# A two-block network on one core: the recurrent stage in 64-column matrices, one 64x64 fp32 tile a head

## What is computed

```python
def step(S, inp):
    r_t, w_t, k_t, v_t, a_t, b_t = inp
    sa = jnp.einsum('bhij,bhj->bhi', S, a_t)
    S = S * w_t[:, :, None, :] + sa[..., None] * b_t[:, :, None, :] + v_t[..., None] * k_t[:, :, None, :]
    return S, jnp.einsum('bhij,bhj->bhi', S, r_t)
...
mean = jnp.mean(y, axis=-1, keepdims=True)
var = jnp.mean(jnp.square(y - mean), axis=-1, keepdims=True)
y = ((y - mean) * lax.rsqrt(var + GN_EPS)).reshape(B, L, D_INNER)
y = y * ln_w.astype(jnp.float32) + ln_b.astype(jnp.float32)
```

## Time and profile before

| | |
|---|---|
| median of the three runs | 2902.48 us |
| profiled execution: its own time | 2891.52 us |
| its span, first to last instruction | 2889.5 us |
| granted clock of TensorE, mean | 0.931 |
| TensorE matmul busy | 2475.3 us (86%) |
| VectorE busy | 1648.8 us (57%) |
| GpSimd busy | 1468.6 us (51%) |
| ScalarE busy | 965.5 us (33%) |

### The profile page before, as it was taken

One profiled execution on the slowest core, in us unless ns is written; L12 is line 12 of the kernel. 1 busy time (PEld: TensorE's weight loads), 2 busy tenths in 40 slices (PEclk: granted clock), 3 DMA queues, 4 the chain that ended last, 5 costly groups with the idle time before them and its releaser, 6 DMA issues.

```text
span 2889.5 us, 45055 instructions
## 1 busy us (share of the span) xinstructions
PE 2475.3 (86%) x15926; PEld 2161.8 (75%) x15926; DVE 1648.8 (57%) x2307; ACT 965.5 (33%) x2235; POOL 1468.6 (51%) x907
## 2 busy tenths in 40 slices
PE   6799999897888887888877869999998689978876
PEld 5689898797787777878877859677778577666555
DVE  6766666667666676666765264144442417337755
ACT  1532323354455454445442122223331111111331
POOL 1466666644443354444338748312218579775334
PEclk8899999898999998889998979999999899989998
DMA  2243434611131212222221212200002222121101
GB/s 83 86 160 140 158 145 148 175 30 42 46 74 42 46 41 42 67 53 44 44 91 50 80 38 86 73 30 29 29 30 59 97 73 87 51 66 59 43 0 58
DMA packets 141815, 201.95 MB, mean 70 GB/s; under 512 B 101888, under 2 KB 104064, under 8 KB 139392
## 3 DMA queue, kind: packets, MB, share of 16 engines
q1 hardware_dynamic: 141696, 200.20, 22.9%
HBM read 161.18 MB, written 38.99 MB: 69 GB/s over the span
## 4 chain that ended last, share of the span: by engine, by line
PE 71%; DVE 17%; issue 6%; ACT 4%; POOL 1%; DVEq 0%; DMA 0%; SPq 0%; ACTq 0%; POOLq 0%
PE wide L1182 10%; PE wide L1183 10%; PE wide L1184 10%; PE wide L770 8%; PE wide L775 5%; PE wide L1666 4%; PE wide L355 4%; PE wide L1762 2%; DVE w_rounded L967 2%; PE wide L1726 1%; PE wide L751 1%; PE wide L1727 1%; PE wide L757 1%; PE wide L1551 1%; PE wide L761 1%
## 5 line engine op out<-in xcount | busy, mean ns | idle before, releaser
L1049 POOL TENSOR_TENSOR n_levels<-n,masks 128x384 fp32r<-128x384 f32 x192 | 201.7, 1079 | 173.7 <-PE wide L770 173.7
L1182 PE MATMUL wide<-mixed_high,w_high_rwkv_in 128*128 128x264 f32 x720 | 212.1, 295 | 29.0 <-ACT log_decay L435 20.1
L1184 PE MATMUL wide<-mixed_high,w_low_rwkv_in 128*128 128x264 f32 x720 | 206.6, 287 | 0.0
L1299 DVE TENSOR_TENSOR sq_sum<-sq_sum,squares 128x528 f32<-128x528 f32 (+1 forms) x54 | 87.3, 1617 | 180.4 <-ACT squares L1264 180.4
L1183 PE MATMUL wide<-u_low_second,w_high 128*128 128x512 f32 x464 | 185.7, 400 | 0.0
L1206 POOL TENSOR_TENSOR w_high<-weights,con 128x1024 fp32r<-128x1024 f32 x60 | 147.3, 2456 | 74.5 <-PE wide L1184 64.6
L958 DVE TENSOR_TENSOR w_rounded<-wide,w_rounded 128x384 fp32r<-128x384 f32 x240 | 124.4, 550 | 97.0 <-PE wide L770 96.7
L355 PE MATMUL wide<-mixed_in,weights 128*128 128x264 f32 x672 | 159.1, 395 | 13.4 <-DVE mixed_in L325 12.0
L1182 PEld LDWEIGHTS wide<-mixed_high,w_high_rwkv_in 128*128 128x128 f32 x720 | 138.2, 192 | 37.2 <-ACT log_decay L435 26.3
L1209 POOL TENSOR_TENSOR w_low<-weights,w_high 128x1024 fp32r<-128x1024 f32 x60 | 157.7, 2628 | 4.7
L355 PEld LDWEIGHTS wide<-mixed_in,weights 128*128 128x128 f32 x672 | 129.1, 194 | 40.8 <-issue 9.5
(11 more groups left out here) (355 smaller groups left out, 7901.9 us busy)
## 6 DMA issues: line engine op xcount, KB each, us to landing
weights<-in_stream SPq DMA_DIRECT2D x200, 512.0 KB, 3.5
forms<-form SPq DMA_DIRECT2D x16, 2020.5 KB, 6.3
a_r<-forms SPq DMA_DIRECT2D x16, 576.0 KB, 5.0
gate_bonus<-forms SPq DMA_DIRECT2D x16, 576.0 KB, 3.9
b_diag<-forms SPq DMA_DIRECT2D x32, 144.0 KB, 5.2
k_diag<-forms SPq DMA_DIRECT2D x32, 144.0 KB, 5.2
v_diag<-forms SPq DMA_DIRECT2D x32, 144.0 KB, 4.9
a_diag<-forms SPq DMA_DIRECT2D x32, 144.0 KB, 4.5
```

What stands on the lines that cost most here:

```text
L1049: pool.tensor_tensor(n_lvl[:, lv % LEVEL_BUFS, grp(g), :], n_all[:, grp(g), :], mask("levels", lv + 1), ALU.mult).then_inc(q["n_level"], 1)
L1182: pe.matmul(dst, w[0], x[0], start=start, stop=False)
L1184: return pe.matmul(dst, w[1], x[0], start=False, stop=stop)
```

## The change

The recurrent stage is rewritten in compact form.

- **Matrices.** Every matrix of a pair is 64 columns wide: the first head on partitions 0 to 63, the second on 64 to 127. No block diagonals, no zeros, no memsets. A product is made once a head, from that head's rows into that head's rows of the same PSUM bank, as a 64x64 tile of the array.
- **Inverse.** E and W are fp32 products. X is no longer a transpose of W: each level also multiplies E and X the other way round (item XW), and one VectorE add of 2 x 192 columns updates both. The correction step (F, V) is gone, and with it GpSimd's L1052.
- **Transposes** become products with a 64x64 unit matrix; N comes from a product of its own in place of a transpose.
- **Order.** M and A move into the pass that inverts. The walk is spread evenly over the whole pass. "rows", M and the normalising products fill the gaps between the E groups.
- **Normalising.** The sum of y comes from the copy's accumulator (ScalarE), the sum of squares from nine ScalarE squares of one chunk each, the last scale and shift from ScalarE.
- **DMAs.** One of 5 x 576 columns replaces the nine for a pair's forms, into two buffers; r comes in one in place of two.
- **Waits.** A semaphore a head is counted; ahead of each group TensorE's queue has an increment that carries the group's waits (`begin`).
- **GpSimd** multiplies 192 columns for level 0 and X's start, and 4 x 192 for levels 1 to 4 at once.

```diff
-            def group(out, lhsT, rhs, g, done):
-                for c in range(GC):
-                    mm = pe.matmul(out[:, c * P:(c + 1) * P], lhsT(g * GC + c), rhs(g * GC + c), start=True, stop=True)
-                mm.then_inc(done, 1)
+            def begin():
+                pe.sem_inc(q["turn"], 1)
+            def by_head(out, lhsT, rhs, start, stop, done=None):
+                for hd, rows in enumerate(HEAD_ROWS):
+                    mm = pe.matmul(out[rows], lhsT[rows], rhs[rows], start=start, stop=stop)
+                    if done:
+                        mm.then_inc(done[hd], 1)
+            def group(out, lhsT, rhs, chunks, done, width=C):
+                chunks = range(NC)[chunks]
+                for n, c in enumerate(chunks):
+                    by_head(out[:, n * width:(n + 1) * width], lhsT(c), rhs(c), True, True, done if n == len(chunks) - 1 else None)
...
+                    begin()
+                    by_head(out_u, xw[:, W_OF + pw, c * C:(c + 1) * C], mv[:, pw, c, :], True, c == 0, u_mm if c == 0 else None)
+                    by_head(out_y, mg[:, pw, c, 1, :], v, True, False)
                     if c > 0:
                         pe.wait_ge(q["s_rows"], 9 * p + c)
+                        begin()
+                        by_head(out_u, a_hat[:, pw, c, :], state, False, True, u_mm)
+                        by_head(out_y, b_r[:, pw, c, :], state, False, False)
+                    by_head(out_s, k_tok[:, pw, c, :], v, True, False)
                 else:
+                    begin()
+                    by_head(out_s, b_tok[:, pw, c, :], u_row, False, True, s_mm)
+                    by_head(out_y, qg[:, pw, c, 1, :], u_row, False, True, y_mm)
...
+                for g in range(GROUPS):
+                    rest += [("G", g, 6), ("N", g, 3)]
+                rest += [("start", g, 0) for g in range(GROUPS)]
+                rest += [("rows", n, 3) for n in range(3)] + [("K", g, 6) for g in range(GROUPS)]
+                filler += [("M", g, 3) for g in range(GROUPS)] + [("rows", n, 3) for n in range(3, 12)]
             if post:
+                rest += [("square", g, 0) for g in range(GROUPS)] + [("norm", 0, 0)]
+                filler += [("post", n, 4) for n in range(2)]
             if inv:
                 for lv in range(LEVELS):
                     for g in range(GROUPS):
+                        rest += [("E", (lv, g), 3)] + filler[:1]
+                        filler = filler[1:]
+                    rest += [("XW", (lv, g), 3 if lv == LEVELS - 1 else 6) for g in range(GROUPS)]
+                rest += [("A", g, 3) for g in range(GROUPS)]
+            rest += filler
...
                 elif item == "XW":
                     lv, g = arg
                     pe.wait_ge(q["e_rows"], 15 * i + 3 * lv + g + 1)
+                    begin()
+                    if lv < LEVELS - 1:
+                        group(inv_bank[g], lambda c: e_all[:, c, :], of(x), grp(g), None)
+                    group(inv_bank[g][:, GC * C:], of(x), lambda c: e_all[:, c, :], grp(g), xw_mm)
...
+                elif item == "square":
+                    act.wait_ge(Y_DVE.sem, Y_DVE.at(pp, 2))
+                    for c in range(NC)[grp(arg)]:
+                        ins = act.activation(y_ln[:, c, :], y_ctr[:, c, :], ACT.Square, accum_out=y_var[:, c:c + 1])
+                    ins.then_inc(Y_ACT.sem, 1)
...
+            sp.dma_start(b_f[:, par_, :], forms[i, :, 0:5 * LP]).then_inc(forms_loaded[par_], 16)
```

More of the change, by code:

```diff
@@ L637, in three, with per_head, wait_heads @@
+        def per_head(name):
+            return [sem(f"b_{name}{hd}") for hd in range(2)]
+        g_mm, k_mm, n_mm, token_mm, m_mm, e_mm, xw_mm, a_mm, u_mm, s_mm, y_mm, y_turned = (per_head(n) for n in (
+            "g_mm", "k_mm", "n_mm", "token_mm", "m_mm", "e_mm", "xw_mm", "a_mm", "u_mm", "s_mm", "y_mm", "y_turned"))
+        def wait_heads(eng, done, count):
+            for one in done:
+                eng.wait_ge(one, count)
         def three(ap):
-            return ap[:, 0:GC * P].rearrange("p (c n) -> p c n", c=GC)
+            return ap[:, 0:GC * C].rearrange("p (c n) -> p c n", c=GC)
@@ L695, in is0, with merged @@
         def is0(i):
             return isinstance(i, int) and i == 0
-        def merged(first, second):
-            out, done = [], [0, 0]
-            total = [max(sum(item[2] for item in part), 1) for part in (first, second)]
-            parts = [list(first), list(second)]
-            while parts[0] or parts[1]:
-                n = 0 if not parts[1] or (parts[0] and done[0] * total[1] <= done[1] * total[0]) else 1
-                name, arg, weight = parts[n].pop(0)
+        def merged(walk, rest):
+            out, done = [], 0
+            total, n = max(sum(item[2] for item in rest), 1), 0
+            for name, arg, weight in rest:
+                while n < len(walk) and n * total <= done * len(walk):
+                    out.append(walk[n])
+                    n += 1
@@ L710, in merged @@
                 out.append((name, arg))
-                done[n] += weight
-            return out
-        NORM_AT = 8
+                done += weight
+            return out + walk[n:]
         def schedule(inv, scan, post):
-            setup, levels, ending, walk, norm = [], [], [], [], []
+            rest, filler = [], []
+            if post:
+                rest += [("centre", 0, 0)]
             if inv:
-                setup = [("G", g, 3) for g in range(GROUPS)] + [("K", g, 3) for g in range(GROUPS)]
-                setup += [("T", g, 2) for g in range(GROUPS)] + [("start", g, 0) for g in range(GROUPS)]
+                for g in range(GROUPS):
[3 more added lines that the diff above has]
+                filler += [("M", g, 3) for g in range(GROUPS)] + [("rows", n, 3) for n in range(3, 12)]
@@ L721, in schedule @@
             if post:
-                setup += [("stats", 0, 0)]
-                norm = [("post", g, 2) for g in range(GROUPS)]
+                rest += [("square", g, 0) for g in range(GROUPS)] + [("norm", 0, 0)]
+                filler += [("post", n, 4) for n in range(2)]
             if inv:
-                setup += [("rows", n, 2) for n in range(NORM_AT)]
-            if post:
-                setup += [("norm", 0, 0)]
-            if inv:
-                setup += [("rows", n, 2) for n in range(NORM_AT, 12)]
@@ L738, in schedule @@
-            return merged(ending, setup) + merged(walk, norm + levels)
+                        rest += [("E", (lv, g), 3)] + filler[:1]
[3 more added lines that the diff above has]
+            rest += filler
+            walk = [("walk", divmod(n, 2)) for n in range(2 * NC)] if scan else []
+            return merged(walk, rest)
+        HALVES = (slice(0, 5), slice(5, NC))
@@ L766, in walk @@
-                    pe.matmul(y_bank[:, 0:P], qg[:, pw, c, 1, :], u_row[:], start=False, stop=True).then_inc(q["y_mm"], 1)
-            def group(out, lhsT, rhs, g, done):
-                for c in range(GC):
-                    mm = pe.matmul(out[:, c * P:(c + 1) * P], lhsT(g * GC + c), rhs(g * GC + c), start=True, stop=True)
-                mm.then_inc(done, 1)
-            def turn(out, src, done):
-                for c in range(GC):
-                    mm = pe.transpose(out[:, c * P:(c + 1) * P], src(c), ident)
-                mm.then_inc(done, 1)
+                    begin()
@@ L790, in pe_pass @@
                 elif item == "K":
[L792 to L794 removed]
+                    if arg < 2:
+                        pe.wait_ge(q["token_rows"], 12 * i + arg + 2)
+                    else:
                         pe.wait_ge(q["mg_made"], GROUPS * i + 1)
[L796 to L801 removed]
+                    begin()
```

521 lines of the change are left out of this document (221 added, 300 removed).

## The result

The changed kernel takes 2806.42 us in the median of four runs (2803.63 to 2808.8), the kernel before in the same measurement 2899.14 (2894.61 to 2905.36). The ratio is 0.9683, 95% interval 0.9662 to 0.9705: 93 us less, where 307 were forecast (2595 us). The time lies above the forecast's own range (2490 to 2700) and inside the wide one (2470 to 2860).

The account below looks back on a forecast made before the run. TensorE, fullest but not full, plus waits and clock: 33 + 1.8 + 0.8 + 3.5 + 1.5 + 3, say 44 us a pass for 61.7. With the ends 310 us less, forecast 2595 us; own range 2490 to 2700, wide 2470 to 2860.

Parts of the forecast that it names:

- The pace of TensorE: Recurrent stage: a pair of 64-column tiles, both heads overlapping, costs 0.112 us; 295 of them make 33 us a pass.
- Rival 1: Recurrent stage: the heads take turns on TensorE, 0.224 us a pair of tiles, 70.5 us a pass, 3018 us; chance 0.12.
- The clock: Recurrent stage: a share of 0.1 to 0.16 at half clock costs about 3 us a pass.
- Rival 2: Recurrent stage: the granted clock stays at 0.5 throughout, every record doubles, 3020 us; chance 0.07.
- What hides ... none is on the path: Each pass: VectorE, GpSimd and ScalarE work stays under TensorE's 33 us; SP's 5 DMAs, 13 before, cost nothing.
- The lump: ScalarE ahead of the first level: nine squares, table load and root make TensorE wait 3.5 us a pass (1 to 6).
- Rival 4: TensorE's queue: the increment ahead of each group drains it, about 0.2 us each, 17 a pass, about 2850 us; chance 0.04.
- the small waits: TensorE's waits outside the lump: 0.8 us at a pass's end and 1.5 (0 to 5) for other short ones.
- Rival 3: Levels: copies, adds and turns don't fit behind one another and the lump is longer; 52 us a pass, 2712; chance 0.15.
- Entry: Start of the recurrent stage: without memsets and diagonal DMAs the first product starts at about 531, 15 us less.
- Pass 0: First pass of the stage: 41.7 us before, 31 with the level's waits after, 10 us less.
- The end: From the loop's end to stage C: the ending's 16 us go, loading and splitting 14 outputs then decides, 20 us less.

Follow-up runs that it names:

- Run 6: On run 4: products of items E and XW move 32 columns in place of 64, same number of instructions, result not the inverse; 2730.12 us.
- run 3: On the changed kernel: gate and bonus get their own semaphore and the next pair's forms are issued ahead of the wait for z; 2720.29 us.
- run 4: On run 3: the nine ScalarE squares are spread behind the E groups of levels 0 to 2, the root put at level 3; 2701.56 us.
- run 9: On run 4: the loop of 7 turns with two passes is written out on all engines but SP, without the branch; 2698.95 us.
- run 5: On run 4: each of the 85 increments a pass on TensorE's queue stands there twice; 2766.05 us.
- run 10: On run 4: 13 of a pass's 85 increments on TensorE's queue go, their waits joined to those of the group ahead; 2665.6 us.
- run 7: On run 4: E and XW take two of each group's three chunks in one product of 128 columns, result not the inverse; 2648.69 us.
- run 8: On run 4: products of E and XW move 128 columns in place of 64, same number of instructions, result not the inverse; 2778.39 us.

## Why the prediction was right or wrong

**The pace of TensorE: right.** A pair of tiles was put at 0.112 us. The timeline at the full clock:

```profile
747.07 0.29 PE L745 MATMUL wide<-m_v,x_w 64*64 64x64 f32 x4
747.18 0.29 PE L745 MATMUL wide<-v_rows_rwkv,k_with_a_r 64*64 64x64 f32 x4
747.30 0.29 PE L745 MATMUL wide<-state,a_hat 64*64 64x64 f32 x4
```

Four records every 0.117 us, 0.029 each; a product with 128 columns takes 0.22. 259 pairs of 64 and 18 of 128 make 34.3 us, forecast 33 (the trace's unbroken rows of products, put at the full clock, come to 34.6). Rival 1 falls: both heads write the same bank, on different partitions, and overlap. In turn a pair would take 0.224, by the forecast's estimate. Run 6 adds what the forecast had only from far rows: at 64 columns this pace is hardly that of the columns any more, so halving them would not have halved it.

**"The clock": nearly right.** The granted clock was 0.90 in the loop. The forecast put 3 us a pass for it, with a share of 0.1 to 0.16 at half clock that was the author's estimate and that no run shows; measured, the rows at half of the clock take 5.1 us a pass, which costs 2.6. Rival 2 falls. The clock rose to 0.96 when the DMA waits went (run 3), so a part of its cost was theirs.

**"What hides ... none is on the path": the step that failed.** The prediction counted SP's DMAs, five in place of thirteen, and looked at the buffer that the forms land in. It did not read the order on SP's queue against the order of the items. z had been made at the start of the levels, and the change moves the normalising products to the last level; all that is queued behind SP's wait for z moved with it. Both facts stand in the diff: `filler` has "post" last, and `sp_z` is ahead of the load of gate and bonus and, by the loop, of the next forms. Forecast 0, measured 8.35 us a pass in waits and 86 us in all by run 3.

**Not on the list at all: the reading of instructions.** The sum took TensorE's products, waits and clock. Some 2,350 instructions a pass where there were 900 were counted as array time only. The stops come to 6.4 us a pass in the changed kernel and to about 8.5 to 9 without its DMA waits (both with what of the loop's turn is under "issue"). A packet of the instruction queue has 16,384 B, 256 records stand between most stops, and TensorE goes on 1.4 us after a packet has landed (median, run 4). The loading is not hidden here, since TensorE runs 256 in 3.6 us. In run 9 the branch's long stops go (at most 2.2 us where they were 3.8) and the time stays (2698.95 us, 2701.56 in run 4).

**The lump: over-sized.** Forecast 3.5 us a pass, bounds 1 and 6. ScalarE's rows show it as described: nine squares at 0.24 each, one every 0.24, then the table load and the root:

```profile
865.62 0.25 ACT L910 ACTIVATE y_ln<-y_centred 128x64 f32<-128x64 f32 x1
865.78 0.19 ACT L910 ACTIVATION_READ_ACCUMULATOR y_ln<-y_centred 128x1 f32 x1
...
867.89 1.28 ACT L914 ACT_TABLE_LOAD   x1
869.19 0.30 ACT L914 ACTIVATE y_var<-y_var,epsilon 128x9 f32<-128x9 f32 x1
```

The nine take 2.3 us, not 2.9, since the accumulator's read lies beside the next square. TensorE waited 1.5 us; spreading it gave 1.4 a pass.

**The increments: rightly at nothing in the rows of products, but not without effect.** Rival 4 falls: its price was 0.2 each, and the rows above show 0.12 from `k_with_a_r` to `state` across an increment, as between pieces without one. A second increment in each place did cost (run 5, 4.5 us a pass), and taking 13 away shortened the stops (run 10, 2.4 us a pass); neither effect was in the sum.

**The pass, added up.** 34.3 of products, 8.35 of DMA waits, 6.4 of issue, 1.5 of the lump and 0.7 of other waits are 51.3 of 56.6. The remaining 5 are the half clock, 2.6, and the drain ahead of each wait and stop, 2.8: from start to start the pauses take 19.3 us, and the idle rows, which begin at a record's end, show 16.5 of them. Against the forecast's 43.6 that is 8.35 for the DMA waits, 4.6 for the issue stops (6.4 where 1.8 stood), 2.8 for the drains and 1.3 for the products too little, and 3.6 too much for the lump and the small waits (2.2 where 5.8 stood) and 0.4 for the clock: 13 together. The sum had no mistake of arithmetic that matters; 2582 and 11 make 2593, not 2595. Rival 3 gave the time of a pass best (52), for another reason: the copies and additions of a level do fit; of its waits only the lump is there.

**The ends: half right.** Entry forecast 15, measured 4: the first product came at 541.67, not 531. The memsets and diagonal loads had run beside VectorE's work on the last pair, and with them gone VectorE's work is what is late:

```profile
533.53 3.46 DVE kk_inv L502
537.01 0.72 DVE kk L504
538.06 0.57 issue
538.63 0.71 DVE kk_inv L512
539.80 0.19 issue
539.99 0.70 DVE form L518
540.70 0.62 DVE form L521
541.34 0.23 DVE eye L1020
```

I had followed one chain and not asked what was next to it. Pass 0: forecast 10, measured 2; three stops of 3.4, 1.7 and 1.6 us of "issue" stand in it. The end: forecast 20, measured 7.4, with 10.98 us of VectorE splitting outputs (L1432) as named.

## What to carry to other kernels

When a change moves a late producer, read the in-order queue of the DMA engine item by item: everything issued behind its wait moves too, and what is needed first belongs ahead of the wait that ends last. When products are made smaller, work out how long 256 of TensorE's instructions will take: at 3.6 us here they arrived 1.1 us too late, at 4.3 us 0.9, and at 5 us mostly in time. Below that, fewer instructions for the same columns pay (run 7), and a bare semaphore increment more or less can count too (runs 5 and 10). And find what was second on every chain that an edit removes.

## What was not expected of the hardware

- TensorE stops after each 256 instructions when they take 3.6 us: 1.1 us each, a quarter of such a stretch. Wider products fill the stops (run 8: twice the columns in 126 of 277 pairs made the products 12.4 us a pass longer and the pass 4.75).
- 64x64 fp32 tiles with 32 moving columns are hardly cheaper than with 64 (0.11 and 0.12 us a pair); with 128 they cost 0.22.
- Halving products' columns made the kernel slower (2702 to 2730 us), with the granted clock in the loop at 0.90 in place of 0.97; why it fell is open.
- One increment between two products costs nothing that the rows show (0.117 us from start to start with and without it). A second one in each place made a pass 4.5 us longer, 0.053 each, a fifth of it by the clock.
